# First feed-forward of a two-block fp32 kernel with its weights stationary, and the other transposes set in pairs

## The reference

```python
# first block (D_MODEL 2048, D_FF 8192, SEQ 256)
x = x + merged @ w_out
x = x + mem_cross_attn(rmsnorm(x, g_mem_q), mem_n, w_mem_q, w_mem_kv, w_mem_o)
hf = rmsnorm(x, g_ff)
x = x + jnp.square(jax.nn.relu(hf @ w_ff1)) @ w_ff2
x = rmsnorm(x, g_final)
# second block
h = _rms_norm(x, attn_norm_2)
x = x + _hybrid_mixer(h, w_in_2, ...)
h = _rms_norm(x, ffn_norm_2)
return x + (jax.nn.silu(h @ w_gate_2) * (h @ w_up_2)) @ w_down_2
```

## Time and profile before

| | |
|---|---|
| time before, median of 3 runs | 2665.16 us (2661.02 to 2665.3) |
| the profiled execution, its own time | 2665.2 us |
| its span in the trace | 2663.4 us |
| granted TensorE clock, mean | 0.998 |
| PE busy | 2639.8 us, 99% |
| PE weight loads | 83% |
| DVE, ACT busy | 64%, 42% |
| DMA | 483.65 MB, mean 182 GB/s |

### The profile page before, as it was taken

The page is one execution under the profiler, slowest core; times in us unless marked ns, Lnnn a source line. Parts: engine busy times, 40 slices in busy tenths (PEclk is TensorE's granted clock), DMA queues, the critical chain, the costliest instruction groups (busy, mean ns, idle before and its releaser), DMA issues. The chain is left out here.

```text
span 2663.4 us, 33801 instructions
## 1 busy us (share of the span) xinstructions
PE 2639.8 (99%) x12292; PEld 2198.8 (83%) x12292; DVE 1716.5 (64%) x2536; ACT 1122.9 (42%) x1469; POOL 7.4 (0%) x43
## 2 busy tenths in 40 slices
PE   9999999999999999999999999999999999999999
PEld 7978888888878888888888778878888888888887
DVE  7668765566767556556655687877765555555555
ACT  5333454534343333333333544454444444444443
POOL 0000000000000000000000000000000000000000
PEclk9999999999999999999999999999999999999999
DMA  7655556555545555555556566544455556555555
GB/s 228 179 158 166 158 158 216 195 183 185 179 141 190 190 191 187 189 189 189 189 189 205 173 191 182 155 134 143 159 189 190 191 191 191 191 192 190 192 189 168
DMA packets 262499, 483.65 MB, mean 182 GB/s; under 512 B 17738, under 2 KB 39172, under 8 KB 262020
## 3 DMA queue, kind: packets, MB, share of 16 engines
q1 hardware_dynamic: 262372, 482.37, 56.7%
q10 hardware_dynamic: 32, 0.01, 0.0%
HBM read 480.22 MB, written 2.10 MB: 181 GB/s over the span
## 5 line engine op out<-in xcount | busy, mean ns | idle before, releaser
L833 ACT ACTIVATE w_split<-w_raw 128x1024 fp32r<-128x1024 f32 (+2 forms) x920 | 960.5, 1046 | 1279.2 <-PE bank L1007 1223.5
L1175 DVE TENSOR_TENSOR w_split<-w_raw,w_split 128x1024 fp32r<-128x1024 f32 (+2 forms) x920 | 1084.6, 1203 | 243.8 <-ACT w_split L833 237.8
L1005 PE MATMUL bank<-w_split,act_a_hi 128*128 128x512 f32 (+2 forms) x2400 | 945.5, 394 | 7.6 <-DVE w_split L1175 4.3
L1007 PE MATMUL bank<-w_split,act_a_lo 128*128 128x512 f32 (+2 forms) x2400 | 926.0, 386 | 0.0
L1006 PE MATMUL bank<-w_split,act_a_hi 128*128 128x512 f32 (+2 forms) x2400 | 924.2, 385 | 0.0
L1005 PEld LDWEIGHTS bank<-w_split,act_a_hi 128*128 128x128 f32 x2400 | 451.9, 188 | 93.5 <-issue 4.3
L1007 PEld LDWEIGHTS bank<-w_split,act_a_lo 128*128 128x128 f32 x2400 | 451.4, 188 | 89.2
L1006 PEld LDWEIGHTS bank<-w_split,act_a_hi 128*128 128x128 f32 x2400 | 452.4, 188 | 82.5
L1005 PE MATMUL bank<-w_split,act_b_hi 128*128 128x512 f32 x1240 | 487.2, 393 | 1.3 <-issue 1.0
L1007 PE MATMUL bank<-w_split,act_b_lo 128*128 128x512 f32 x1240 | 483.2, 390 | 0.0
L1006 PE MATMUL bank<-w_split,act_b_hi 128*128 128x512 f32 x1240 | 482.7, 389 | 0.0
(11 more groups left out here) (198 smaller groups left out, 962.5 us busy)
## 6 DMA issues: line engine op xcount, KB each, us to landing
w_raw<-in_w_ff SPq DMA_DIRECT2D x256, 512.0 KB, 4.3
w_raw<-in_w_in SPq DMA_DIRECT2D x208, 512.0 KB, 3.8
w_raw<-in_w_gate SPq DMA_DIRECT2D x88, 512.0 KB, 4.0
w_raw<-in_w_up SPq DMA_DIRECT2D x88, 512.0 KB, 4.6
w_raw<-in_w_down SPq DMA_DIRECT2D x88, 512.0 KB, 4.7
w_raw<-in_w_out SPq DMA_DIRECT2D x64, 512.0 KB, 4.0
w_raw<-in_w_in SPq DMA_DIRECT2D x24, 368.0 KB, 3.2
w_raw<-in_w_dsa_o SPq DMA_DIRECT2D x16, 512.0 KB, 4.9
```

The lines of the kernel that those rows point to most:

```text
L833: nc.scalar.activation(whi[:, s, 0:w], raw[:, s, 0:w], ACT.Copy).then_inc(hi_ready, 1)
L1005: pe.matmul(o, hi[:, cols], rhs_hi, start=k == 0, stop=False)
L1007: ins = pe.matmul(o, lo[:, cols], rhs_hi, start=False, stop=k == c["kt"] - 1)
L1175: v_e.tensor_tensor(wlo[:, s, 0:w], raw[:, s, 0:w], whi[:, s, 0:w].bitcast(F32), ALU.subtract).then_inc(lo_ready, 1)
```

## The change

1. **The first feed-forward is turned round.** In the 128 groups of `w_ff1` the weights are the stationary operand and x streams by. `act_a` is laid out so that the high and the low part of one tile of x are 512 columns side by side. For each of four features (128 columns of the chunk) and each k there is `w_hi*[x_hi|x_lo]`, 512 columns, and `w_lo*x_hi`, 256 columns: 16 products in a group instead of 12, with as many columns in all. The result has the features on the partitions, so these chunks have no turns.
2. A chunk takes four banks: the `fa` chunks banks 0 to 3, the `fb` chunks 4 to 7. It is emptied by an item `U` in four parts: ACT copies the low half of each bank (0), DVE adds the high half and takes ReLU times itself (1), ACT rounds to `act_b_hi` (2), DVE subtracts for `act_b_lo` (3). The norm's factor, squared, is applied when `w_ff2` is added to `xres`.
3. Where the four banks come from two chunks that have just been made (`banks_of`), group 0 does only the two features whose banks are free; group 1 does its own for these, waits for the other chunk, and then does the other two features of both.
4. **All other turns stand two together** (lists in a list for `weave`, `pairs()`), which moves them and their neighbours by a group or two.

```diff
+
+
+def pairs(steps):
+
+    return [steps[i:i + 2] for i in range(0, len(steps), 2)]
...
-    seq += weave(mo[2], [squares(0, mo[0])] + hf[:2], 1) + weave(mo[3], [squares(1, mo[1]), squares(2, mo[2])] + hf[2:4], 1)
-    pend = hf[4:6] + [squares(3, mo[3])] + hf[6:]
+    seq += weave(mo[2], [squares(0, mo[0]), hf[:2]], 1) + weave(mo[3], [squares(1, mo[1]), squares(2, mo[2]), hf[2:4]], 1)
+    pend = [hf[4:6], squares(3, mo[3]), hf[6:]]
...
     def up(i, half, **more):
-        return gemm("w_ff1", 0, (2 * i + half) * CH, KT, "A", ev="relu2", rstd="h", step=(0, 2 * CH), rows=True, **more)
-
-    fa, fb = up(0, 0, need=filled(hf)), up(0, 1)
-    seq += weave(fa, pend + [("rstd", dict(of="x", name="h"))], 2)
-    ta = turns(fa, "B", 0)
-    seq += weave(fb, ta, 3)
+        return gemm("w_ff1", 0, (2 * i + half) * CH, KT, "A", step=(0, 2 * CH), kind="up", half=half, **more)
+
+    def activated(c):
+        return [("U", dict(chunk=c, part=i)) for i in range(4)]
+
+    fa, fb = up(0, 0, need=filled(hf), banks_of=mo[2:4]), up(0, 1, banks_of="aux")
+    seq += weave_up(fa, pend + [("rstd", dict(of="x", name="h", square=True))], 2)
+    seq += weave_up(fb, activated(fa), 1)
...
-    tb = turns(fb, "B", 4)
-    fa, fb2 = up(1, 0), up(1, 1)
-    body += weave(fa, tb, 3)
-    down_need = filled(ta + tb)
-    for m in range(4):
-        body += weave(gemm("w_ff2", 0, m * CH, 8, "B", 0, need=down_need if m == 0 else (), ev="addx", off=m * CH,
-                           step=(2 * CH, 0)))
-    ta2 = turns(fa, "B", 0)
-    body += weave(fb2, ta2, 2)
+    fa, fb2 = up(1, 0, banks_of="up"), up(1, 1)
+    body += weave_up(fa, activated(fb), 1)
+    downs = [gemm("w_ff2", 0, m * CH, 8, "B", 0, need_up=[(0, fb)] if m == 0 else (), ev="addx", off=m * CH, scaled=True, bank0=4,
+                  step=(2 * CH, 0)) for m in range(4)]
+    for c in downs:
+        body += weave(c)
+    fb2["banks_of"] = downs[2:4]
+    body += weave_up(fb2, activated(fa), 1)
     turns_ff = FF // (2 * CH)
     segments.append((body, turns_ff - 1))
...
+    ub = activated(fb2)
     seq = [("load_gain", {})]
     distances = [("distances", dict(part=i)) for i in range(8)]
-    down = [gemm("w_ff2", (turns_ff - 1) * 2 * CH, m * CH, 8, "B", 0, need=filled(ta2 + tb) if m < 2 else (),
-                 ev="addx", off=m * CH, rows=True) for m in range(4)]
+    down = [gemm("w_ff2", (turns_ff - 1) * 2 * CH, m * CH, 8, "B", 0, need_up=[(0, fa), (2, fb2)] if m == 0 else (),
+                 ev="addx", off=m * CH, scaled=True, rows=True) for m in range(4)]
     xt = [turn("x", 2 * i * P, "A", 2 * i, down[i // 2], gain="attn_norm_2", nth=i + 1) for i in range(8)]
     twice = [("twice", dict(m=m, rows=down[m])) for m in range(4)]
     (a0, a1, a2, a3), (b0, b1, b2, b3) = groups_of(down[0]), groups_of(down[1])
-    seq += [a0, b0, tb[0], a1, tb[1], b1, distances[0], a2, distances[1], a3, ("E", down[0]), b2, distances[2], b3, ("E", down[1])]
-    seq += weave(down[2], [squares(0, down[0])] + xt[:2] + [distances[3], twice[0]], 1)
-    seq += weave(down[3], [squares(1, down[1]), xt[2], squares(2, down[2]), xt[3]] + distances[4:6] + [xt[4], twice[1]], 1)
-    pend = [squares(3, down[3]), xt[5], distances[6], twice[2], twice[3], xt[6], ("rstd", dict(of="x", name="f")), distances[7],
-            xt[7], ("rstd", dict(of="x2", name="h"))]
+    seq += [a0] + ub[:2] + [b0] + ub[2:] + [a1, b1, distances[0], a2, distances[1], a3, ("E", down[0]), b2, distances[2], b3, ("E", down[1])]
+    seq += weave(down[2], [squares(0, down[0]), xt[:2], distances[3], twice[0]], 1)
+    seq += weave(down[3], [squares(1, down[1]), xt[2:4], squares(2, down[2])] + distances[4:6] + [xt[4], twice[1]], 1)
+    pend = [squares(3, down[3]), xt[5:7], distances[6], twice[2], [twice[3], xt[7]], ("rstd", dict(of="x", name="f")), distances[7],
+            ("rstd", dict(of="x2", name="h"))]
...
+            def up_group(c, i, s, turn):
+
+
+                of, early, late = c["banks_of"], (0, 1), (2, 3)
+                if i == 0 and of == "up":
+                    wait(pe, up_out, c["v"] - 1, turn.v)
+                elif i == 0 and of == "aux":
+                    for j in (c["last_j"] - 1, c["last_j"]):
+                        pe.wait_ge(aux_out[j % 2], j // 2 + 1)
+                elif not isinstance(of, str) and i < 2:
+                    x = of[i]
+                    if of[0]["c"] % 2:
+                        early, late = late, early
+                    if i == 0:
+                        wait(pe, chunk_out[x["c"] % 2], x["c"] // 2 + 1, turn.c2)
+                        up_part(c, 0, s, early)
+                        return
+                    up_part(c, 1, s, early)
+                    wait(pe, chunk_out[x["c"] % 2], x["c"] // 2 + 1, turn.c2)
+                    up_part(c, 0, (s - 1) % RING, late).then_inc(group_done, 1)
+                    up_part(c, 1, s, late).then_inc(group_done, 1)
+                    return
+                up_part(c, i, s, early + late).then_inc(group_done, 1)
+
+            def up_part(c, i, s, features):
+                for f in features:
+                    o = bank[4 * c["half"] + f]
+                    for kk in range(2):
+                        k = 2 * i + kk
+                        w = slice(kk * CH + f * P, kk * CH + (f + 1) * P)
+                        if kk == 0:
+                            pe.matmul(o[:, :], whi[:, s, w], act_a[:, k].rearrange("p s t -> p (s t)"), start=k == 0, stop=False)
+                        ins = pe.matmul(o[:, SEQ:2 * SEQ], wlo[:, s, w], act_a[:, k, 0], start=False, stop=False)
+                        if kk == 1:
+                            ins = pe.matmul(o[:, :], whi[:, s, w], act_a[:, k].rearrange("p s t -> p (s t)"), start=False, stop=k == KT - 1)
+                return ins
+
...
                 elif ev == "addx":
                     for t in range(NT):
                         x = xres[:, t, c["off"]:c["off"] + CH]
-                        ins = v_e.tensor_tensor(x, b[t], x, ALU.add)
+                        if c.get("scaled"):
+                            ins = v_e.scalar_tensor_tensor(x, b[t], s_("rstd_sq", t, t + 1), x, ALU.mult, ALU.add)
+                        else:
+                            ins = v_e.tensor_tensor(x, b[t], x, ALU.add)
                     ins.then_inc(out_sem, 1)
-                elif ev == "relu2":
...
+            def activated(what, turn):
+
+                half, v = what["chunk"]["half"], what["v"] + 1
+                u = stage[:, half].rearrange("p t c -> p (t c)")
+                if what["part"] == 1:
+                    wait(dve, up_lows, v, turn.v)
+                    for f in range(4):
+                        uf = u[:, f * SEQ:(f + 1) * SEQ]
+                        ins = v_e.tensor_tensor(uf, bank[4 * half + f][:, 0:SEQ], uf, ALU.add)
+                    step(ins)
+                    v_e.scalar_tensor_tensor(u, u, 0.0, u, ALU.max, ALU.mult).then_inc(up_squared, 1)
+                elif what["part"] == 3:
+                    hi, lo = (x[:, half * 4 * SEQ:(half + 1) * 4 * SEQ] for x in act["B"])
+                    wait(dve, up_hi, v, turn.v)
+                    v_e.tensor_tensor(lo, u, hi.bitcast(F32), ALU.subtract).then_inc(up_out, 1)
+
```

More of the change, by code:

```diff
@@ L112, in weave, with weave_up @@
     return [x for item in out for x in (item if isinstance(item, list) else [item])]
+def weave_up(c, side, start):
+    return weave(c, side, start)[:-1]
 def lead(c, steps, ahead=2):
@@ L240, in plan @@
     part = cut(steps, 4)
[L241 removed]
+    part[0] = [turns(qb[1], "qb", 4, scale=SCALE)] + part[0]
     for i in range(4):
@@ L363, in plan @@
     steps, o_fox = attention([dict(kind="fox", q="qf", kk="kf", v="vf", h=h, kh=h, k=h) for h in range(8)])
-    part = cut(late + steps[:4] + pend + steps[4:], 4, (2, 5, 5, 5))
+    part = cut(late + steps[:4] + pairs(pend) + steps[4:], 4, (2, 5, 5, 5))
     for i in range(4):
@@ L477, in number @@
                         what["ref_" + k] += per[k] * (reps - 1)
+                if "ref_end" in what and (id(what), "end") not in seen:
+                    seen.add((id(what), "end"))
+                    what["ref_end"] += per["g"] * (reps - 1)
             turn_groups = groups[at:]
@@ L866, in leave @@
                 ins.then_inc(chunk_out[c["c"] % 2], 1)
+            def activated(what, turn):
+                half = what["chunk"]["half"]
+                u = stage[:, half].rearrange("p t c -> p (t c)")
+                if what["part"] == 0:
+                    wait(act_e, group_done, what["end"], turn.g)
+                    for f in range(4):
+                        ins = nc.scalar.activation(u[:, f * SEQ:(f + 1) * SEQ], bank[4 * half + f][:, SEQ:2 * SEQ], ACT.Copy)
+                    ins.then_inc(up_lows, 1)
+                elif what["part"] == 2:
+                    wait(act_e, up_squared, what["v"] + 1, turn.v)
+                    nc.scalar.activation(act["B"][0][:, half * 4 * SEQ:(half + 1) * 4 * SEQ], u, ACT.Copy).then_inc(up_hi, 1)
```

(14 more changed lines are left out.)

108 lines of the change are left out of this document (57 added, 51 removed).

## The result

The changed kernel takes 2649.45 us, the median of 4 runs (2648.1 to 2650.72), against 2665.23 before; the ratio is 0.9946, interval 0.9932 to 0.9959. The forecast was 2648.6. The profiled execution of the changed kernel took 2649.4 us with a span of 2647.6, 15.8 less than before.

A forecast was written before the change was run, and what follows sets the result against it. TensorE, busy for 99% of the span, was taken to bound the kernel, so edits count by what they take off its stream and waits. Terms summed to -16.6 us, from 2665.16 to 2648.6 us; range 2640 to 2660.

The forecast's parts named there:

- turns of the first feed-forward gone: First feed-forward: 32 turns at 0.49 us each leave PE's path, -15.7 us.
- its products: Turned groups of the first feed-forward: 2.77 us each against 2.72, over 128 groups +6.4 us.
- entry: Entry of the feed-forward: PE waits 2.2 us for mo[3] in xres, then slow-clock products; +3.8 us, from +2.2 to +4.6.
- norm ahead of `w_in_2`: Ahead of w_in_2: waits of 1.18 and 2.17 us and eight slow products go, -5.0 us; -1.2 if only the first.
- nsa heads: Among the nsa heads: wait of 3.37 us shrinks to 1.9 without slow products, -3.7 us; -1.5 if the clock falls.
- indexer: Indexer's chunk: four turns in a row behind group 71 wait for banks, +0.9 us, from +0.5 to +2.
- pairs elsewhere: 47 more places with two turns together, each saving 0.05 to 0.09 us: -3.3 us, from 0 to -4.2.
- Rival (a): Turned groups: weight loads bound narrow products, 0.19 us instead of 0.12; +72 us, about 2720; chance 0.05.
- Work on ACT and DVE: Turned chunks: extra ACT and DVE work is covered, act_b ready about 5 us before w_ff2 asks; costed at nothing.
- rival (b): Feed-forward loop: the wait for four banks returns each turn, seven times; +15 to +27 us, 2664 to 2675; chance 0.08.
- Rival (c): Pairs make DVE late elsewhere; waits at norm and heads stay or move, pairs save nothing; 2658 us; chance 0.18.
- Rival (d): Turned groups: narrow products at half price, and no slow clock at the entry; 2640.6 us; chance 0.07.

The follow-up runs named there:

- e2: The first feed-forward turned round as in the changed kernel, all other turns single where they stood before; 2658.85 us, ratio 0.9984 to the kernel before.
- e4b: Changed kernel with all wide products of a turned group first, then all narrow ones; 2649.09 us, a group 2.793.
- e5: Changed kernel with wide and narrow products by turns within each feature; 2655.5 us, a group 2.818 to 2.831.
- e6: Changed kernel with 192 columns instead of 256 in each narrow product, part of the result left out; 2641.42 us in one run, a group 2.720.
- e3: Changed kernel with two turns of x moved behind the evacuation of mo[3] at the feed-forward's entry; 2646.37 us, ratio 0.9941 to the kernel before.
- e1: Changed kernel with the first feed-forward and its single turns as before, all other turns in pairs; 2653.13 us, ratio 0.9966 to the kernel before.
- e7: Changed kernel with the old order of turns and norms ahead of w_in_2 put back; 2653.91 us in one run.

## Why the prediction was right, point by point

The time is 0.85 us above the forecast, and the terms stand so:

| term | forecast | measured |
|---|---|---|
| turns of the first feed-forward gone | -15.7 | -15.4, by their price before |
| its products | +6.4 | +8.6 |
| entry | +3.8 | +3.6 |
| norm ahead of `w_in_2` | -5.0 | -5.7 |
| nsa heads | -3.7 | -4.2 |
| indexer | +0.9 | +0.8 |
| pairs elsewhere | -3.3 | -3.3, pairs and small waits together |

The first two rows can't be told apart in the changed trace, where the turns are gone: the first is 32 times the 0.48 us that a turn costs in the trace of before, the second the length of a turned group. Together they are -6.8, which is what e2 shows without its wait.

*Turns.* 32 at 0.48 instead of 0.49. Right.

*Products.* The one term that was mis-sized: 0.067 x 128, a third more. The step that had the wrong size is "8 x 0.2267 + 8 x 0.1196 = 2.77 us": prices of streams of one width were added for a mixed stream. The narrow ones came at 0.115 and the wide ones at 0.233. That the mixed stream might have a price of its own was said, and put at nothing. e4b and e5 show that the order moves it, by 0.006 and 0.04 a group.

*Rival (a)* did not happen, but it is nearer than the forecast had it. The 0.19 us that a load is shown busy bounds nothing; a floor near 0.108 fits (e6), and the narrow products lie 8 ns above it.

*Pairs.* A pair costs 0.89 or 0.92 where two singles cost 0.96, so it saves 0.04 to 0.07; the 0.05 to 0.09 of the forecast was a little high. The four stretches away from the named places have 38 of the 47 new pairs. By that price these are worth -2.1. The waits in those stretches became 2.1 us shorter as well, most of them for `s_sb`, which was not forecast, and 0.9 us came back in places that were not traced. So the mechanism was right, and that the two totals agree at -3.3 is in part luck. Nor do all other turns stand two together, as the change has it: in the changed trace 50 places have two, one has four, and 16 turns still stand alone.

*Work on ACT and DVE.* No wait for `up_out` in any list, and with it the argument against rival (b): PE waited for a chunk's four banks once, not eight times. In the loop DVE has the last part of an item `U` done at 860.0 and PE's first product of `w_ff2` starts at 864.7, the cover of 5 us that was forecast.

*Entry.* Mechanism, place and length are right: 2.04 against 2.2, DVE done at 797.1 against 797.7, PE ready at 795.1 against 795.5. e3, which takes the wait away, gives 3.8 back in its trace and 3.1 in the medians. What was wrong in kind is the price of the clock. I laid 2.2 beside 2.17 and 1.94 and took the length to decide. It doesn't: 2.0 was followed by slow products in two profiles and not in four. Both profiles of the changed kernel have them, and seven of its nine executions have a mean clock that tells of a slow stretch somewhere, so the sum was right by a draw.

*Norm and heads.* Both waits went by the order of the items and by nothing else (e1 and e2, and e7 for the norm), -5.7 and -4.2; 1.6 and 2.2 of these are slow products that are not there in every execution of the kernel before. That the forecast, made from one profiled execution, meets the median is therefore in part luck too: that execution lies at the median of before, and most executions of both kernels have their slow stretches. Among the heads the forecast said a wait of 1.9, it is 1.72.

*Indexer.* The size was right and its make-up was not: the four turns in a row cost 0.3 and not 0.8, groups 62 to 68 cost 1.1, and a wait of 0.64 in group 80, which I had not counted, went (0.9 with what it drew after it).

*Rival (c)* named 2658 for pairs that make DVE late. They did so at the entry, by 0.5 us (the wait is 1.5 in e2 and 2.0 with pairs), and in the indexer's chunk, by two waits of 0.35 us for a bank. *Rival (d)* did not happen: the products cost 8.6 us, not nothing, and the entry had its slow products in both profiles.

## What to carry over

Where one engine is full, price an edit by the starts of its instructions and walk the queue of the engine that it waits for, one entry after the other; here that gave the large waits, new and vanished, to a few tenths of a microsecond; of the small ones it missed some. Read the price of a stream from a stream with the same neighbours: short instructions make the ones behind them dearer. It paid to put transposes together; it did not pay to put all narrow products of a group together (e4b), and it cost to spread them out one by one (e5). When banks or buffers come to be shared with work that has just ended, put its evacuation ahead of everything else that the emptying engine has there.
